# Conv part of the output projection: two groups taken side by side, and one bias moved

## What is computed

```python
mod = jax.nn.silu(c) @ w_ada + b_ada
sh1, sc1, g1, sh2, sc2, g2 = jnp.split(mod[:, None, :], 6, axis=-1)
h = rms_norm(x, norm_mix_g) * (1 + sc1) + sh1
proj = h @ w_in                      # c_q, c_kv, k_r, u, g_b, g_c
gated_in = g_c * u
conv = (conv_w[0] * ext[:, :S] + conv_w[1] * ext[:, 1:S + 1]
        + conv_w[2] * ext[:, 2:S + 2] + conv_b)
y_conv = g_b * conv
mix = jnp.concatenate([attn.reshape(B, S, D_ATTN), y_conv], axis=-1) @ w_out
x = x + g1 * mix
```

## Time and profile before

| what | value |
|---|---|
| time before, median of 3 runs | 1391.7 us (1390.52 to 1393.0) |
| profiled execution | 1394.74 us, span 1392.9 us |
| TensorE busy | 1356.6 us, 97% of the span |
| VectorE, ScalarE, GpSimd busy | 909.4, 452.7, 49.6 us |
| TensorE's waits of over 0.5 us, from 186 to 340 us | four, 4.5 us in all |
| granted TensorE clock, mean | 0.994 |

### The profile page before, as it was taken

One profiled execution on the slowest core, in us unless ns is written; L12 is line 12 of the kernel. 1 busy time (PEld: TensorE's weight loads), 2 busy tenths in 40 slices (PEclk: granted clock), 3 DMA queues, 4 the chain that ended last, 5 costly groups with the idle time before them and its releaser, 6 DMA issues.

```text
span 1392.9 us, 23608 instructions
## 1 busy us (share of the span) xinstructions
PE 1356.6 (97%) x9524; PEld 1276.1 (92%) x9524; DVE 909.4 (65%) x1430; ACT 452.7 (33%) x737; POOL 49.6 (4%) x57
## 2 busy tenths in 40 slices
PE   7899999999999999999999999999999999999996
PEld 4599999999997666789999999999999999999996
DVE  6789988282655567777866565655555565656566
ACT  4532221133302334445741322323232313232223
POOL 0000000000012112100000000000000000000000
PEclk9999999999999999999999999999999999999999
DMA  9344444531213222030111211011111211121203
GB/s 370 106 136 136 139 138 106 212 88 33 89 29 88 84 75 43 1 108 17 46 47 46 61 30 60 30 60 36 55 60 30 75 30 60 45 60 30 60 30 125
DMA packets 112952, 107.14 MB, mean 77 GB/s; under 512 B 9552, under 2 KB 97192, under 8 KB 112128
## 3 DMA queue, kind: packets, MB, share of 16 engines
q1 hardware_dynamic: 110288, 105.09, 24.8%
q10 hardware_dynamic: 2608, 1.28, 0.3%
HBM read 88.93 MB, written 9.88 MB: 71 GB/s over the span
## 4 chain that ended last, share of the span: by engine, by line
PE 87%; DVE 7%; DMA 2%; SPq 1%; ACT 1%; issue 1%; POOL 0%; DVEq 0%; POOLq 0%; ACTq 0%
PE PS L1180 29%; PE PS L1198 17%; PE PS L765 14%; PE PS L1090 4%; PE PS L944 4%; PE PS L1070 3%; PE PS L1302 3%; PE PS L1128 2%; PE PS L1281 1%; PE PS L1017 1%; PE PS L864 1%; DMA ADA<-in_w_ada 1%; DVE ACC L1956 1%; PE PS L818 1%; PE PS L1037 1%; PE PS L972 1%
## 5 line engine op out<-in xcount | busy, mean ns | idle before, releaser
L2342 DVE TENSOR_TENSOR EL<-HALF_W,EH 128x512 fp32r<-128x512 f32 x163 | 112.1, 688 | 122.7 <-ACT EH L1621 121.8
L1621 ACT ACTIVATE EH<-HALF_W 128x512 fp32r<-128x512 f32 x163 | 102.2, 627 | 256.9 <-PE PS L1198 151.3
L2478 DVE SCALAR_TENSOR_TENSOR X<-PS,MOD,X 128x792 f32<-128x792 f32 (+2 forms) x240 | 125.4, 578 | 70.3 <-PE PS L1198 70.3
L1180 PE MATMUL PS<-HBL_T,EH 128*128 128x264 f32 x640 | 169.7, 285 | 0.0
L1180 PE MATMUL PS<-HBH_T,EH 128*128 128x264 f32 x640 | 169.4, 285 | 0.0
L1198 PE MATMUL PS<-AL,EH 128*128 128x264 f32 x640 | 162.7, 285 | 0.0
L1198 PE MATMUL PS<-AH,EH 128*128 128x264 f32 x640 | 162.3, 284 | 0.0
L765 PE MATMUL PS<-HH,WH 128*128 128x352 f32 x432 | 140.5, 326 | 3.3 <-DVE WL L1911 2.3
L765 PE MATMUL PS<-HL,WH 128*128 128x352 f32 x432 | 139.8, 324 | 0.0
L1180 PE MATMUL PS<-HBH_T,EL 128*128 128x264 f32 x640 | 130.1, 284 | 0.0
L1180 PE MATMUL PS<-HBL_B,EH 128*128 128x264 f32 x480 | 127.2, 285 | 0.0
(11 more groups left out here) (328 smaller groups left out, 2854.9 us busy)
## 6 DMA issues: line engine op xcount, KB each, us to landing
ADA<-in_w_ada SPq DMA_DIRECT2D x22, 1024.0 KB, 5.4
HALF_W<-in_w_gate SPq DMA_DIRECT2D x22, 512.0 KB, 3.8
HALF_W<-in_w_up SPq DMA_DIRECT2D x22, 512.0 KB, 3.9
HALF_W<-in_w_down SPq DMA_DIRECT2D x22, 512.0 KB, 3.7
RAW<-in_w_in SPq DMA_DIRECT2D x20, 512.0 KB, 6.5
x_saved_rows<-X SPq DMA_DIRECT2D x2, 2112.0 KB, 14.1
X<-x_saved_rows SPq DMA_DIRECT2D x4, 1056.0 KB, 5.7
out<-ORW SPq DMA_DIRECT2D x8, 512.0 KB, 2.7
```

Source lines behind the costliest of these rows:

```text
L1180: mm = pe.matmul(PS[:, 2 * s + n, 0:HQ], w, x[:, k, n * HQ:(n + 1) * HQ], start=(first and w is wh and x is xh), stop=(ends and w is wl), ...
L1621: act.activation(dst if len(src.shape) == 2 else dst.rearrange("p (k c) -> p k c", k=2), src, ACT.Copy)\
L2342: dve.tensor_tensor(el, src, eh.bitcast(F32), ALU.subtract).then_inc(entry_lo, 1)
L2478: ins = dve.scalar_tensor_tensor(dst, src, MOD[:, G2 + m, st:st + 1], dst, ALU.mult, ALU.add)
```

## The change

Four things are changed.

- TensorE: for g13 and g14, steps 0, 1, 2 of both come first, then the first gather, then step 3 of g13 and of g14. Groups g15 to g20 are as they were.
- VectorE: the bias of columns 40 to 47 stands behind the sum of SSK and not behind the memsets.
- SP: COS and SIN wait for the last of the sixteen reductions (`acc_summed` at 18, with the two that it starts with) and not for the bias (`mod_kept`).
- SP: WQ waits for the second gather (`ada_turned` at 6).

```diff
-            sp.wait_ge(mod_kept, 3)
+            sp.wait_ge(acc_summed, 18)
             sp.dma_start(COS[:], c_cos).then_inc(tables_loaded, 16)
             sp.dma_start(SIN[:], c_sin).then_inc(tables_loaded, 16)
...
+                    sp.wait_ge(ada_turned, 6)
                     sp.dma_start(WQ[:], w_uq[0].rearrange("(k p) m -> p k m", p=P)).then_inc(wq_loaded, 16)
...
-            def before_out(k):
-
-                if k == NJ - 1:
-                    gather_sums(7, 0, 12)
-                pe.wait_ge(y_lo, k + 2)
-
-            for n in range(4):
+            begin_slot(S_COUT)
+            for m in range(2):
+                begin_group(G_COUT + m)
+                for k in range(NJ - 1):
+                    if m == 0:
+                        pe.wait_ge(y_lo, k + 2)
+                    step(G_COUT + m, weights_of(S_COUT, NJ, m), y, k, k == 0, False)
+            gather_sums(7, 0, 12)
+            pe.wait_ge(y_lo, NJ + 1)
+            for m in range(2):
+                step(G_COUT + m, weights_of(S_COUT, NJ, m), y, NJ - 1, False, True)
+            for n in range(1, 4):
                 begin_slot(S_COUT + n)
                 for m in range(2):
                     g = G_COUT + 2 * n + m
                     begin_group(g)
-                    product(g, weights_of(S_COUT + n, NJ, m), y, range(NJ), before=before_out if n + m == 0 else None)
+                    product(g, weights_of(S_COUT + n, NJ, m), y, range(NJ))
...
-            dve.wait_ge(ada_turned, 6)
-            add_late_bias(6, 40, 8, 3)
             split_lo(S_CKV + 1)
...
+            dve.wait_ge(ada_turned, 6)
+            add_late_bias(6, 40, 8, 3)
             g = G_KR
```

## The result

Over 20 executions each, the changed kernel took 1394.39 us (median; 1393.2 to 1397.04) and the kernel before 1392.77 us. The ratio, which leaves out one time of before (3984 us), is 1.0016 with a 95% interval of 1.0009 to 1.0023: the change made the kernel 2.2 us slower (1.3 to 3.2), within the 0.2% that I called the same. The two medians by themselves lie 1.6 us apart. The forecast was 1392.6 us and +0.87.

A forecast was written before the change was run, and what follows sets the result against it. TensorE bounds the kernel, busy for 1356.6 of 1392.9 us. The terms -1.37 - 1.67 + 5.56 + 1.67 - 0.15 - 1.59 - 1.58 = +0.87 us, added to the median 1391.7, gave 1392.6 us; range 1389.7 to 1395.2.

The forecast's parts named there:

- (1): At g13 and g14, the wait for y goes: 1.37 us of wait and 1.67 of low clock gained.
- (2): Before g15, a new TensorE wait of 5.56 us for VectorE's emptying of g13, behind the late gather.
- Part (5): At the second latent group, the moved bias gains 1.59 us of wait and 1.58 us of clock.
- part 6: On SP, the moved loads end no TensorE wait, so there is no gain.
- part 4: Behind g15, VectorE, 3.16 us late, catches up: 10.7 us per two groups against TensorE's 11.6; a 0.15 us wait goes.
- part 3: Behind the new wait at g15, low clock costs 1.67 us, bounded from 0 to 3.3.
- the prediction's own sign of being wrong: Behind the new wait at g15: the clock staying low past 216 us, where 212 to 216 was expected.
- The estimate of 2.1 us: Low clock cost from g15's start at 212.41: half the time until the clock's return, making the sum 0.4 higher.
- Rival B: The pause before g15 costs no clock: -0.8 us, 1390.9 us, still the same; chance 0.13.
- the row at 53.08: A 2.30 us wait at 53.08 us, with clock 1.00 at 53 to 55 us, read as costing no clock.
- Rival C: Low clock lasts over all of g15, 5.8 us more: +5.0 us, 1396.7 us; chance 0.08.
- Rival A: The new wait before g15 doesn't show and all the rest is gain: 6.4 us, 1385.3 us; chance 0.07.

The follow-up runs named there:

- experiment 3: The changed kernel with 30 useless matmuls added on TensorE between the last step of g14 and g15: 1392.59 us, ratio 0.9995 to the kernel before.
- experiment 4: The changed kernel with the first gather moved back behind g13's three steps: 1390.65 us, ratio 0.9978 to the kernel before.
- experiment 1: The kernel before with only the moved bias and SP's two new waits, TensorE's order as before: 1389.99 us, ratio 0.9976.
- experiment 7: Experiment 1 with the rotary tables' loads and all behind them on SP held until the second gather: 1388.99 us, ratio 0.9973 to the kernel before.
- experiment 6: The changed kernel with VectorE emptying g13 and g14 ahead of the first weighted sum: 1394.52 us, ratio 1.0016 to the kernel before.
- experiment 2: The changed kernel with the bias and SP's waits put back, only TensorE's order new: 1398.62 us, ratio 1.0034 to the kernel before.
- experiment 5: Experiment 4 with VectorE emptying groups in the middle of its weighted sums: 1388.14 us, ratio 0.997 to the kernel before.

## Why the prediction was right, and where it was off

**Right: the new wait.** Parts (1) and (2) said that g15 would start 18.17 us after the first step, with a wait of 5.56 us. It was 18.17, with 5.52 or 5.53, in three profiles, and 18.17 also in experiment 3. Experiment 4 shows the cause: undo the gather's lateness, and the wait falls by 3.16 us.

**Right: the moved bias.** Part (5) gave 3.17 us; the profile shows 3.31 (15.78 to 12.47), and experiment 1 by itself 3.3 faster.

**Right: nothing for the loads** (part 6, experiment 7) **and the catching up of VectorE** (part 4): no wait at g17 or g19, but by 0.9 us of slack per pair only, which experiment 6 shows from the other side.

**Mis-sized: the clock behind the new wait (part 3).** I took 1.67 us, from the waits of 1.37 and 1.59. It was 2.35, 1.5 and 2.8 in three profiles, 2.2 in the mean. In those short waits the clock fell only after TensorE had resumed; in the long one it was down to 0.50 before, and stayed so for 5.0, 3.1 and 6.0 us of work. In the first and the third of these it was low past 216 us, the prediction's own sign of being wrong. The Trainium skill ("TensorE: Matmul & The Clock Gate", section "What's actually happening") has the low clock as the default that activity lifts. The traces agree: the clock fell in the pause of 5.5 us, and stayed at 1.00 when matmuls filled it (experiment 3). The estimate of 2.1 us that I worked out by that rule was nearer than the row I went by. Rival B (no fall) did not happen in any of four long pauses, and the row at 53.08 that spoke for it was one of the three profiles in 13 where that wait passed. Rival C (the low clock over all of g15) did not happen either; the highest cost was 2.8 us, where C began at 3.6.

**Mis-sized: the falls that the change removes.** I counted 1.67 and 1.58 us as if every execution of before had both. Experiments 2 and 7 show executions with one missing, and experiment 7 that the first is worth 0.6 us on the path when it comes: VectorE frees g13 no sooner. In my sum this stood in the start of g15 (209.87), so the sum was right for that execution, but not for one without the falls. Rival A's 6.4 us has the same fault: the profile of experiment 5 bears it out against a profile with both falls (6.29 us), the medians give 4.2.

**The sum again, and what was luck.** With the parts as measured it is (18.17 - 15.63) + (46.4 + 2.2 - 46.76) + (12.47 - 15.78) = 2.54 + 1.84 - 3.31 = +1.1 us against an execution of before that has both falls. One without the second fall is 1.5 us shorter (14.25 against 15.78, experiment 2), one without the first 0.6 us. If they are missing as often as in the table, in 1 of 4 and 1 of 5, that adds some 0.5 us: an estimate of +1.6, inside the measured 1.3 to 3.2. The forecast's +0.87 is outside it. "The same" was right, but with 0.6 us to spare and not 1.9. Luck had its part: the clock term was 0.68 us too small in the first profile, and two small terms err the other way and hide half of that (the wait of 0.15 us had cost 0.36, and the moved bias gave 3.31 for 3.17). The bound of no cost at all rested on a wait that the clock happened to pass. The forecast of the time itself, 1392.6 us, also started from a median of three times (1391.7) that was 1.1 us under the later one of 20 (1392.77).

**Rival A** (no new wait) was refuted by the rows. Experiment 5 is the kernel that it would have needed.

## What to carry to other kernels

When a small operation is moved back on TensorE to hide a wait, look at who waits for its result and what is queued behind that wait: here 1 us of gather held up 8 us of VectorE work, the last of which freed TensorE's own banks. VectorE, with 0.9 us of slack in 11.6, could not take up a sum of 6.3 us that was put off, because the bank was needed two groups later; putting the work off only moved the wait. And one profile is one execution: a spell of low clock behind a wait of 1.4 to 2.3 us, and its absence too, should go into a sum with a chance, not as a fixed price.

## What was not expected of the hardware

- Behind the same short wait (1.37 or 1.59 us, the same within 0.01 us in each profile) the clock falls to 1.2 GHz in most executions and not in others: 7 of 9. With the wait of 2.30 us at 51 to 53 us it is 10 of 13. A wait of 2.37 us at g15 passed at 2.4 GHz in the one profile that has it (experiment 4).
- The low clock behind a pause of 5.5 us cost 1.5, 2.35 and 2.8 us in three executions of the same instructions. Thirty useless matmuls in the pause took it away (experiment 3): 2.9 us less.
- Low clock can be hidden in large part. Behind the YL wait 1.55 us of matmul time were lost and 0.6 us of it reached the path (15.62 against 15.02 us).
